# A hybrid decoder layer on one core: the first norm's column factors loaded as one row and spread by two products

## The reference

```python
def rmsnorm(x, g):
    xf = x.astype(jnp.float32)
    r = lax.rsqrt(jnp.mean(xf * xf, axis=-1, keepdims=True) + RMS_EPS)
    return (xf * r * g.astype(jnp.float32)).astype(x.dtype)

def swiglu(x, w_gate_up, w_down):
    gu = x @ w_gate_up
    g, u = jnp.split(gu, 2, axis=-1)
    return (jax.nn.silu(g) * u) @ w_down

h = x + 0.5 * swiglu(rmsnorm(x, ffn1_norm), ffn1_w_gate_up, ffn1_w_down)
...
h = h + 0.5 * swiglu(rmsnorm(h, ffn2_norm), ffn2_w_gate_up, ffn2_w_down)
out = rmsnorm(h, final_norm)
```

## Time and profile before

| | us |
|---|---|
| median of 3 runs | 1925.39 |
| lowest and highest of them | 1924.86, 1926.58 |
| the profiled execution, its own time | 1925.05 |
| its span, first to last instruction | 1923.1 |
| PE busy in the span | 1911.5 |
| DVE busy | 1391.7 |
| ACT busy | 787.4 |
| POOL busy | 151.0 |

### The profile page before, as it was taken

The page is one execution under the profiler, slowest core; times in us unless marked ns, Lnnn a source line. Parts: engine busy times, 40 slices in busy tenths (PEclk is TensorE's granted clock), DMA queues, the critical chain, the costliest instruction groups (busy, mean ns, idle before and its releaser), DMA issues.

```text
span 1923.1 us, 25205 instructions
## 1 busy us (share of the span) xinstructions
PE 1911.5 (99%) x9046; PEld 1599.1 (83%) x9046; DVE 1391.7 (72%) x1714; ACT 787.4 (41%) x1170; POOL 151.0 (8%) x221
## 2 busy tenths in 40 slices
PE   9999999999999999999999999999999999999998
PEld 9888888888888888888888888898888888888887
DVE  6977867774566776786878878879767777755555
ACT  7423232323434543345665652464323232324344
POOL 1000000000000300002443420010000000000002
PEclk9999999999999999999999999999999999999999
DMA  5456654558675534248446347633536454677655
GB/s 165 145 200 229 226 172 150 188 195 309 216 236 194 184 110 153 72 131 236 144 128 173 102 153 249 198 137 110 186 133 202 142 177 146 217 263 248 205 193 205
DMA packets 246723, 347.19 MB, mean 181 GB/s; under 512 B 16368, under 2 KB 150256, under 8 KB 243056
## 3 DMA queue, kind: packets, MB, share of 16 engines
q1 hardware_dynamic: 246640, 346.10, 54.6%
HBM read 232.79 MB, written 112.98 MB: 180 GB/s over the span
## 4 chain that ended last, share of the span: by engine, by line
PE 97%; DVE 2%; issue 0%; ACT 0%; DMA 0%; POOL 0%; SPq 0%; POOLq 0%; DVEq 0%; ACTq 0%
PE bank L1231 39%; PE bank L1328 11%; PE bank L1275 9%; PE bank L1276 9%; PE bank L1277 9%; PE bank L1187 5%; PE bank L1469 4%; PE bank L1377 2%; PE bank L1405 2%; PE bank L1435 2%; PE bank L1540 2%; PE bank L1162 1%; PE bank L1559 1%; PE bank L1558 1%; PE bank L1525 1%; PE bank L1523 1%
## 5 line engine op out<-in xcount | busy, mean ns | idle before, releaser
L2168 DVE TENSOR_TENSOR dn_lo<-dn_lo_raw,dn_hi 128x1024 fp32r<-128x1024 f32 x149 | 181.6, 1222 | 149.2 <-ACT dn_hi L1738 148.9
L1231 PE MATMUL bank<-hi_t,wa_hi 128*128 128x512 f32 x640 | 249.0, 389 | 0.2 <-issue 0.2
L1231 PE MATMUL bank<-lo_t,wa_hi 128*128 128x512 f32 x640 | 249.0, 389 | 0.0
L1231 PE MATMUL bank<-hi_t,wa_lo 128*128 128x512 f32 x640 | 249.0, 389 | 0.0
L1738 ACT ACTIVATE dn_hi<-dn_lo_raw 128x1024 fp32r<-128x1024 f32 x149 | 157.9, 1061 | 216.9 <-DMA dn_lo_raw<-act_dram 216.8
L1275 PE MATMUL bank<-dn_hi 128*128 128x512 f32 x596 | 232.5, 390 | 0.0
L1276 PE MATMUL bank<-dn_hi,dn_lo 128*128 128x512 f32 x596 | 231.9, 389 | 0.0
L1277 PE MATMUL bank<-dn_lo,dn_hi 128*128 128x512 f32 x596 | 231.9, 389 | 0.0
L1231 PE MATMUL bank<-hi_b,wa_hi 128*128 128x512 f32 x480 | 186.8, 389 | 0.5 <-DVE up L2292 0.5
L1231 PE MATMUL bank<-lo_b,wa_hi 128*128 128x512 f32 x480 | 186.7, 389 | 0.0
L1231 PE MATMUL bank<-hi_b,wa_lo 128*128 128x512 f32 x480 | 186.7, 389 | 0.0
(11 more groups left out here) (275 smaller groups left out, 3761.6 us busy)
## 6 DMA issues: line engine op xcount, KB each, us to landing
wa_lo_raw<-in_ffn_w_gate_up_dram SPq DMA_DIRECT2D x87, 512.0 KB, 4.9
dn_lo_raw<-act_dram SPq DMA_DIRECT2D x149, 256.0 KB, 4.1
act_dram<-g SPq DMA_DIRECT2D x44, 512.0 KB, 4.5
wd_t<-in_ffn_w_down_dram SPq DMA_DIRECT2D x44, 512.0 KB, 6.6
act_dram<-s_of SPq DMA_DIRECT2D x88, 256.0 KB, 6.4
wd_dram<-wd_t SPq DMA_DIRECT2D x22, 1024.0 KB, 5.8
dn_lo_raw<-wd_dram SPq DMA_DIRECT2D x85, 256.0 KB, 3.3
dn_lo_raw<-in_ffn_w_down_dram SPq DMA_DIRECT2D x64, 256.0 KB, 3.0
```

The source lines that it names most:

```text
L1231: last = nc.tensor.matmul(acc, lhs, rhs, start=n == 0 and i != 2 and i < 5, stop=n == 11, skip_group_check=True)
L2168: return nc.vector.tensor_tensor(dst, raw, hi.bitcast(f32), ALU.subtract)
```

## The change

The gain of the first norm no longer comes as 128 copies. SP loads the vector once, as one row of 4 KB on one partition (`gain_row`), in the place in the queue where the 512 KB stood. POOL fills a row of 128 ones (`ones_row`) on the same partition, with one more memset ahead of the identity. PE transposes 10 blocks of zeros, waits for the row, and multiplies the column of ones by each half of the row: a product over a single partition, f32 by f32, of 128 x 512, which puts the half row on all 128 partitions of a bank. Banks 1 and 2 hold the two halves. ACT copies the first from PSUM to `gain` after square(0) (`take_gain`), DVE the second.

DVE scales tile 0 in two instructions of 512 columns each: the first half, then its copy of the second half of the gain, then the second half. `xn_ok` is raised after the last, so PE's transpositions of tile 0 wait for all three. The other three norms load the gain as before; for them the semaphore `gain_in` counts the same, since the two copies add 8 each.

PE's transpositions of zeros go from 36 to 10 + 14 around the two products, from 16 to 6 and from 10 to 6. Two pairs of semaphores are merged to make room: `quarter_in` into the row's `rows_in` (a later wait for 32 becomes one for 48), `wghi` and `wglo` into `wg_split`; later waits on `const_set` are one higher.

```diff
+        ones_row = at("ones_row", [1, P], f32, base + 194 * K + 512)
+        gain_row = at("gain_row", [1, DM], f32, base + 188 * K)
...
                 if t == 0:
-                    load_gain(0)
+                    sp_.dma_start(gain_row[:, :], gains[0]).then_inc(rows_in, 16)
...
-            pe.wait_ge(const_set, 4)
-            keep_busy(36)
+            pe.wait_ge(const_set, 5)
+            keep_busy(10)
+            pe.wait_ge(rows_in, 16)
+            for half in range(2):
+                nc.tensor.matmul(bank[:, 1 + half, :], ones_row[:, :], gain_row[:, half * HALF:(half + 1) * HALF],
+                                 start=True, stop=True).then_inc(row_spread, 1)
+            keep_busy(14)
             transposes(0, 0)
-            keep_busy(16)
+            keep_busy(6)
             transposes(0, 1)
-            keep_busy(10)
+            keep_busy(6)
...
+            def take_gain():
+
+                act.wait_ge(row_spread, 1)
+                nc.scalar.activation(gain[:, 0:HALF], bank[:, 1, :], ACT.Copy).then_inc(gain_in, 8)
...
             square(0, 0)
+            take_gain()
             square(0, 1)
...
-            scale_rows(0, 0)
+            for half in range(2):
+                part = slice(4 * half, 4 * half + 4)
+                if half:
+                    dve.wait_ge(row_spread, 2)
+                    nc.vector.tensor_copy(gain[:, HALF:], bank[:, 2, :]).then_inc(gain_in, 8)
+                dve.wait_ge(rstd_ok, 1)
+                dve.wait_ge(gain_in, 8 * (half + 1))
+                last = nc.vector.scalar_tensor_tensor(out=xn_rows(0, 0)[:, part], in0=as_rows(h_tile(0, 0))[:, part],
+                                                      scalar=rstd[:, 0, 0:1], in1=as_rows(gain[:, :])[:, part],
+                                                      op0=ALU.mult, op1=ALU.mult)
+            last.then_inc(xn_ok, 1)
             scale_rows(0, 1)
...
+            nc.gpsimd.memset(ones_row[:, :], 1.0).then_inc(const_set, 1)
-            pool.wait_ge(const_set, 3)
+            pool.wait_ge(const_set, 4)
```

More of the change, by code:

```diff
@@ L416, in macaron_layer @@
         half_in = sem("half_in")
-        quarter_in = sem("quarter_in")
+        rows_in = sem("rows_in")
         head_in = [sem(f"head_in{i}") for i in range(2)]
@@ L460, in macaron_layer @@
         wpiece = sem("wpiece")
-        wghi = sem("wghi")
-        wglo = sem("wglo")
+        wg_split = sem("wg_split")
+        row_spread = sem("row_spread")
         mb_in = sem("mb_in")
@@ L1005, in load_head @@
                     for half, part in ((top, 0), (low, 1)):
-                        sp_.dma_start(q_st[half, slot, c0:c1].bitcast(f32), qk_dram[part, pair, rows, c0:c1]).then_inc(quarter_in if hn == 0 and c0 == 0 else landed, 16)
+                        sp_.dma_start(q_st[half, slot, c0:c1].bitcast(f32), qk_dram[part, pair, rows, c0:c1]).then_inc(rows_in if hn == 0 and c0 == 0 else landed, 16)
             def load_v(pair):
@@ L1386, in group_quad @@
                 pe.wait_ge(ylo, 2 * m + 2)
-                pe.wait_ge(wglo, 1)
+                pe.wait_ge(wg_split, 2)
                 for b in range(4):
@@ L1514, in logits @@
                 if n == FIRST_LOW and part == 0:
-                    pe.wait_ge(quarter_in, 32)
+                    pe.wait_ge(rows_in, 48)
                 if c in (0, 1):
@@ L2025, in _ @@
             act.wait_ge(mb_add, 5 * NM)
-            nc.scalar.activation(wg_hi[:, :, :], wg_raw[:, :, :], ACT.Copy).then_inc(wghi, 1)
+            nc.scalar.activation(wg_hi[:, :, :], wg_raw[:, :, :], ACT.Copy).then_inc(wg_split, 1)
             pool_hi(0, 1)
@@ L2680, in pool_tile @@
                 dve.wait_ge(mb_add, 5 * NM)
-                dve.wait_ge(const_set, 6)
+                dve.wait_ge(const_set, 7)
                 if gi:
@@ L2703, in group_weights_lo @@
             def group_weights_lo():
-                dve.wait_ge(wghi, 1)
+                dve.wait_ge(wg_split, 1)
                 nc.vector.tensor_tensor(wg_lo[:, :, :].rearrange("p g d -> p (g d)"),
@@ L2708, in group_weights_lo @@
                                         wg_hi[:, :, :].rearrange("p g d -> p (g d)").bitcast(f32),
-                                        ALU.subtract).then_inc(wglo, 1)
+                                        ALU.subtract).then_inc(wg_split, 1)
             def pool_weight_sums(u):
```

## The result

| | before | after |
|---|---|---|
| median of 12 runs | 1925.33 | 1929.82 |
| lowest and highest | 1924.86, 1926.68 | 1928.28, 1931.59 |
| the profiled execution, its own time | 1925.05 | 1928.28 |
| its span | 1923.1 | 1926.4 |

All times are in us. The ratio after to before is 1.0024, with a 95% interval of 1.0016 to 1.0031: 4.5 us slower. The interval leaves out 1, and the ratio itself lies just beyond the 0.2% that the prediction took for what can be told from no change. The forecast was 1925.9 us, its range 1924.8 to 1927.3 us, and "within 0.2%" had a chance of 0.96. Sign right, size far too small, range missed.

What follows compares the result with a forecast made beforehand. PE, busy 1911.5 of 1923.1 us, bounds the kernel, so only its stream's start at 18.58 us matters. Tile 0's longer chain, partly absorbed, moves it +0.6 us: 1925.65 us profiled, forecast 1925.9 us as median, range 1924.8 to 1927.3 us.

Steps and rivals of the forecast that it cites:

- the sum: Program head: tile 0 scaled 1.2 us later, gate weights' low half +0.59 us, PE's stream from 19.2 us, +0.6 us.
- VectorE's tail: VectorE from the gate weights' low half to PE's stream: unbroken and still 7.26 us long, so it carries the start.
- the upper end: Each f32 product on PE costs four fp32r ones: 0.90 us at full clock, the first 1.81 us.
- The rival of cheap products: PE's products take one or two passes, or the clock rises sooner: +0.05 us, 1925.4 us; chance 0.20.
- the second 0.90 us if the clock rises when it did: Second product on PE: at full clock, as the rise stays near 6.3 us; it ends at 7.27 us.
- PE's fourteen transpositions after the products end at 7.27 + 14 x 0.11 = 8.8 us and are in nobody's way: Zeros on PE behind the products: 0.11 us each at full clock, done before tile 0 is scaled at 9.13 us.
- The clock rises late: Rival at the head: PE's clock rises near 8.2 us or later after a short pause, 1926.6 or 1928.3 us; chance 0.17.
- second branch: Late clock rising only after all fourteen transpositions: ACT's copy near 12.2 us, low half near 14.2 us, +2.9 us, 1928.3 us.
- the lost clock: Rival: PE's wait before its first real matmul loses the clock, the stream's 6.02 us double, some 1931 us; chance 0.03.
- the latest rise: The late clock's latest case, rise only after all fourteen transpositions: +2.9 us, 1928.3 us; left out of the range.

Runs made afterwards that it cites:

- after_full: Kernel after with the two products over 128 partitions, the row in partition 0 of a block of zeros; median 1927.52 us, ratio 1.0011 to before.
- gap_in_before: Kernel before with its first 36 transpositions of zeros replaced by 10, a wait for the first square's sum, and 12 more; 1925.96 us, ratio 1.0002.
- no14: Kernel after without the fourteen transpositions of zeros between the products and tile 0; median 1928.97 us, ratio 1.0017 to before.
- zeros_first: Kernel after with 22 transpositions of zeros ahead of the products in place of 10; median 1928.46 us, ratio 1.0015 to before.
- full_wahi: after_full with ACT's high half of the gate weights moved ahead of tile 0's high halves; median 1926.71 us, ratio 1.0005 to before.
- short_row: Kernel after with the row first rounded to fp32r by DVE, so one-pass products, still over one partition; median 1927.60 us, ratio 1.0014 to before.

## Why the prediction was wrong

**Right: what bounds, and the frame of the sum.** "The whole effect of this change on the time is by how much the start at 18.58 us moves": most of it. VectorE's tail carried the start as foreseen, 7.27 us against 7.26. The row landed in time for a product at 4.31 us (4.55 foreseen), the second x tile at 5.9 us (5.9), the copy of the gain began at 6.48 us (6.45), the first half scale at 7.19 us (7.1). The half scales took 0.75 us (0.74 from the rows), the copy 0.69 us (0.60). Where the clock rises early, in after_full, the sum comes true up to the stream's start: tile 0 scaled at 8.49 + 0.75 = 9.24 us (9.13), hi_b at 9.99 (9.88), the low half at 12.05 (11.91), the stream at 19.32 (19.2). The time of after_full, 1927.52 us, still lies above the forecast, by what it loses behind the head.

**Right: the length of a product.** The view of line L1358 of after (count, ns min/median/max, first and last start, shape):

```profile
L1358 PE MATMUL bank<-gain_row,ones_row x4: 1056/1056/1214, 4.3 to 7.0; 1*128 1x512 f32 x4
```

Each product shows as two records, and the four start (7.0 - 4.3) / 3 = 0.9 us apart: 1.8 us a product at 1.2 GHz, the upper end that was taken (1.81). The rival of cheap products falls. The Trainium skill's page "FP8 and Floating Point Precision", section TensorE Precision Notes, has four passes for true FP32; an estimate by it, 4 x 512 columns at 1.2 GHz, is 1.71 us, and this trace agrees within 0.1 us.

**Wrong: "the second 0.90 us if the clock rises when it did"**, and with it "PE's fourteen transpositions after the products end at 7.27 + 14 x 0.11 = 8.8 us and are in nobody's way". I took the moment of the rise, 6.3 us, from a stretch of transpositions of 128 partitions and let it stand when two thirds of that stretch were replaced by work of another shape. The clock did not rise in the products at all, so the second cost 1.8 us like the first, and the fourteen ran at 0.22 us each to 11.06 us, as filler ahead of tile 0. Tile 0 was scaled 0.6 us behind the forecast (9.74 for 9.13) and then stood 1.3 us behind the filler. From there every step is late by the same amount: hi_b 1.87 us, low half 1.90, stream 1.88 us behind the forecast. In the other two profiles the rise was still later, and the start 22.2 us.

**The rival had the mechanism and not the trigger.** "The clock rises late" gave for its second branch 12.2, 14.2 us and +2.9 us; the first profile has 11.75, 13.81 us and +2.4 us against the mean start of before, the others +3.6 and +3.5 us, as even tile 0's transpositions ran slow. I gave it 0.17 because I hung it on a pause of 0.3 us, which the earlier trace rows made look harmless. The first profile of after shows no such pause, and one of 1.36 us is harmless (gap_in_before). That the shape of the product could matter wasn't weighed, though no row of before has a product over one partition: the product's length was bounded from both sides, its effect on the clock was not. The range then cut off exactly this branch ("it leaves out the lost clock and the latest rise").

**The lost clock fell.** PE idles 1.51 us before its first real matmul in after, about the 1.6 us foreseen, and the eight matmuls behind it take 1.22 us, the 48 of the stream 6.03 us against 6.02 before.

**Left open: most of 0.8 us behind the head.** The rest of the span averages 1905.0 us in six profiles of before and of its variants (1904.5 to 1905.5) and 1905.8 us in eight of after and its variants (1905.1 to 1906.3). Part of it shows as short waits for loads and for what follows them, such as this one in PE's timeline of after, 0.29 us for a load of `q_st`:

```profile
876.99 0.50 PE L1530 MATMUL bank<-k_hi,q_st 128*128 128x512 f32 x1 [0.29 <-DMA q_st<-qk_dram]
```

But a variant without the load of one row has the like; the timeline of PE in gap_in_before:

```profile
875.90 0.50 PE L1525 MATMUL bank<-k_hi,q_st 128*128 128x512 f32 x1 [0.26 <-DMA k_lo<-qk_dram]
```

One wait goes with the late start. In the three profiles of after, in no14 and in zeros_first, whose streams start at 20.8 us or later, PE's weight load near 1343 us waits 0.5 us for VectorE's `up`; in the other nine, which start by 20.4 us, it waits 0.2 us. The timelines of PE's weight loads, after and then before:

```profile
1342.80 0.19 PEld L1233 LDWEIGHTS bank<-hi_b,wa_hi 128*128 128x128 f32 x1 [0.52 <-DVE up L2305]
```

```profile
1339.53 0.19 PEld L1231 LDWEIGHTS bank<-hi_b,wa_hi 128*128 128x128 f32 x1 [0.17 <-DVE up L2292]
```

Counted from the stream's start, these five lose 0.4 us against before over the stretch from some 1290 to 1350 us, the others less than 0.1 us. The merged semaphores alone don't cause this, since after_full, full_wahi and short_row have them and don't lose it. Why a late start makes this wait longer was not found. The rest differs from profile to profile, the two groups overlap in it, and no run here says what costs it.

## What to carry to other kernels

Filler that raises PE's clock is part of the program: when some of it is replaced, ask whether the replacement raises the clock too, and don't carry the old moment over. Products over one partition, issued at the low clock, did not: in six of six profiles it rose only at 11.1 us or later. With products over 128 partitions, 127 of them zero, it rose near 5.6 and 8.3 us. And where a wait is about to be removed, look first at the other operand: here it ended 0.14 us sooner, so that the trick had next to nothing to win and three instructions and a clock to lose.

## What was not expected of the hardware

- **Few partitions and the clock.** With one-partition products in PE's first 8.5 us at the low clock, it rose near 11.1, 13.7, 13.0, 13.6, 12.6 and 12.5 us; without them, or with full ones, near 6.3, 6.5, 7.9, 8.4, 7.0, 5.6 and 8.3 us. Once the clock was up, 2.08 us of such products didn't take it away (zeros_first). Both operands of a product lay on the same number of partitions in every run, so which of them counts isn't known, and numbers between 1 and 128 weren't tried.
- **The granted clock of the windows view read 1.00 through all of this**, in before as in after from 8.0 to 11.0 us; only the lengths of equal instructions showed the level.
- **A wait on SP holds up the loads behind it.** In after_full SP waits for VectorE's memset before it loads the row, and x tile 1, next in its list, is issued at 2.39 us where after issued it at 1.63 us. It lands at 7.8 us where after had it at 5.9 us. This fell into slack: ACT waited for PE behind that tile's square. Why the landing is later by more than the issue was not looked into.
